# The SSD layer of a three-block fp32 kernel: ScalarE's slot re-ordered, the C B products and the causal product moved ahead, a GpSimd DMA moved to the head of its slot

## The reference, cut

```python
z, xbc, dt = jnp.split(h @ w_in, ...)
xbc = jax.nn.silu(causal_depthwise_conv(xbc, conv_w, conv_b))
xs, b_in, c_in = jnp.split(xbc, ...)
dt = softplus(dt + dt_bias); a = -jnp.exp(a_log)
a_cs = jnp.cumsum(dt * a)                       # per head, over tokens
decay = jnp.exp(where(causal, a_cs[l] - a_cs[s], -inf))
cb = einsum('bclgn,bcsgn->bcgls', c_c, b_c)     # C B, one per group
y = einsum(cb * decay, xs * dt) + ... + xs * d_skip
g = y * jax.nn.silu(z)
g = g * rsqrt(mean(g * g, over the group) + EPS) * norm_g
out = g @ w_out
```

## Time and profile before

| | |
|---|---|
| median of 3 runs | 1184.22 us (1183.47 to 1185.12) |
| the profiled execution, its own time | 1182.7 us |
| its span, first to last instruction | 1181.0 us |
| TensorE busy | 1124.5 us (95%) |
| VectorE, ScalarE, GpSimd busy | 761.9 (65%), 673.3 (57%), 164.9 us (14%) |
| TensorE's mean granted clock | 0.986 of full speed |
| first layer's slots 0 to 7 | from about 26 to 224 us |
| weight stream | 343 loads of 512 KB, 3.3 us to landing (median) |
| `acs_bc` loads by GpSimd | 8 of 544 KB, 4.8 us to landing (median) |

### The profile page before, as it was taken

How to read it: one execution, slowest core, us unless ns; L and a number is a source line. 1 busy time by engine, 2 the same in 40 slices (tenths; PEclk the granted TensorE clock), 3 DMA queues, 4 the chain that set the end, 5 groups by cost and what they waited for, 6 DMA issues and landing times.

```text
span 1181.0 us, 23759 instructions
## 1 busy us (share of the span) xinstructions
PE 1124.5 (95%) x8898; PEld 1078.7 (91%) x8898; DVE 761.9 (65%) x1119; ACT 673.3 (57%) x1071; POOL 164.9 (14%) x122
## 2 busy tenths in 40 slices
PE   6999999999999999789889999999999999999998
PEld 5888988889999999676579999999998999999998
DVE  4788777857665555458848665555688677666453
ACT  4788887755555443478736555444554656555332
POOL 0434354226100000300002000000001212000000
PEclk8999999999999999989989999999999999999999
DMA  5554434384555555322216555565543555655552
GB/s 194 178 176 152 144 132 155 140 231 166 179 176 178 170 170 176 125 72 92 88 37 195 183 190 183 176 195 176 170 157 127 176 184 173 196 180 192 183 189 93
DMA packets 53225, 190.32 MB, mean 161 GB/s; under 512 B 5920, under 2 KB 7072, under 8 KB 53168
## 3 DMA queue, kind: packets, MB, share of 16 engines
q1 hardware_dynamic: 51408, 182.95, 46.6%
q0 software_dynamic: 1760, 6.59, 1.8%
HBM read 188.44 MB, written 1.08 MB: 160 GB/s over the span
## 4 chain that ended last, share of the span: by engine, by line
PE 73%; issue 10%; DVE 8%; ACT 5%; POOL 3%; DMA 1%; POOLq 0%; ACTq 0%; DVEq 0%; SPq 0%
PE lin L412 23%; PE lin L414 23%; PE lin L413 22%; DVE w_lo L1221 2%; POOL w_lo L1753 2%; ACT w_hi L835 1%; POOL y L1771 1%; DVE cv L1300 1%; PE lin L643 1%; PE ps L445 1%; PE lin L645 1%; ACT pr L1109 0%; DMA acs_bc<-acs_dram 0%; ACT pr L1148 0%; DVE sg L1310 0%
## 5 line engine op out<-in xcount | busy, mean ns | idle before, releaser
L1221 DVE TENSOR_TENSOR w_lo<-w_raw,w_hi 128x1024 fp32r<-128x1024 f32 (+2 forms) x319 | 396.0, 1243 | 282.6 <-ACT w_hi L835 282.5
L835 ACT ACTIVATE w_hi<-w_raw 128x1024 fp32r<-128x1024 f32 (+1 forms) x343 | 354.4, 1040 | 248.6 <-PE lin L414 245.8
L412 PE MATMUL lin<-x_hi,w_hi 128*128 128x256 f32 (+1 forms) x1528 | 444.5, 291 | 11.0 <-DVE x_lo L1247 3.7
L414 PE MATMUL lin<-x_hi,w_lo 128*128 128x256 f32 (+1 forms) x1528 | 438.3, 287 | 0.0
L413 PE MATMUL lin<-x_lo,w_hi 128*128 128x256 f32 (+1 forms) x1528 | 437.6, 286 | 0.0
L412 PEld LDWEIGHTS lin<-x_hi,w_hi 128*128 128x128 f32 x1528 | 291.3, 191 | 15.1 <-DVE x_lo L1247 4.1
L413 PEld LDWEIGHTS lin<-x_lo,w_hi 128*128 128x128 f32 x1528 | 290.8, 190 | 1.4 <-issue 1.0
L414 PEld LDWEIGHTS lin<-x_hi,w_lo 128*128 128x128 f32 x1528 | 291.6, 191 | 0.0
L414 PE MATMUL lin<-hid_hi,w_lo 128*128 128x256 f32 (+1 forms) x768 | 218.2, 284 | 0.0
L413 PE MATMUL lin<-hid_lo,w_hi 128*128 128x256 f32 (+1 forms) x768 | 217.9, 284 | 0.0
L412 PE MATMUL lin<-hid_hi,w_hi 128*128 128x256 f32 (+1 forms) x768 | 217.4, 283 | 0.0
(11 more groups left out here) (251 smaller groups left out, 1481.1 us busy)
## 6 DMA issues: line engine op xcount, KB each, us to landing
w_raw<-w SPq DMA_DIRECT2D x343, 512.0 KB, 3.3
acs_bc<-acs_dram POOLq DMA_DIRECT2D x8, 544.0 KB, 4.8
bias_mask<-rpb POOLq DMA_DIRECT2D x4, 512.0 KB, 10.1
h<-h SPq DMA_DIRECT2D x4, 272.0 KB, 4.3
out<-h SPq DMA_DIRECT2D x8, 128.0 KB, 3.2
cst<-const SPq DMA_DIRECT2D x1, 784.0 KB, 8.8
vecs<-vec SPq DMA_DIRECT2D x1, 131.5 KB, 2.2
acs_dram<-y POOLq DMA_DIRECT2D x1, 34.0 KB, 2.2
```

The lines of the kernel that those rows point to most:

```text
L412: mm3(o, wh, xh, start=first and i == 0, stop=False)
L414: ins = mm3(o, wl, xh, start=False, stop=last and i == kts - 1)
L835: a(w_hi[pg.slot][:, 0:n], w_raw[pg.slot][:, 0:n], ACT.Copy).then_inc(w_hi_done, pages)
L1221: tt(w_lo[pg.slot][:, 0:n], w_raw[pg.slot][:, 0:n], w_hi[pg.slot][:, 0:n].bitcast(F32), ALU.subtract)\
```

## The change

On TensorE the C B products of a running slot are issued before the x transposes. On ScalarE the slot begins with the decay exponentials and the z sigmoid; `conv0` of xs stands between the two `w_hi` of chunk c+2; the square `h_sq` follows the second; the first half of `decay_logs` stands ahead of the xs sigmoid (in slots 1 to 7), the second half ahead of `w_hi` (c+4,0); `w_hi` (c+3,0) stands behind the xs sigmoid; the B C sigmoid stands ahead of `g_hi`. On VectorE the causal product stands ahead of the xs convolution, and the silu of xs ahead of `w_lo` (c+3,0). On GpSimd the DMA of the logarithms stands at the head of the slot. No instruction is added or removed.

```diff
@@ TensorE slot @@
                 if has_scan:
+                    cb_products(s + (-1))
                     x_transposes(s + (-1))
-                    cb_products(s + (-1))
@@ ScalarE slot @@
-                if has_lin:
-                    hi((c + 2).page(0))
-                    hi((c + 2).page(1))
                 if has_scan:
                     decay(g, 0)
                     decay(g, 1)
+                    kz = g.times(3, K_GRP + 2)
+                    act.wait_ge(drained[kz.parity], kz.half + 1)
+                    sigmoid(z_sg[:, :, :], zg_step, g.times(3), z_raw[:, :, :])
+                if has_lin:
+                    hi((c + 2).page(0))
+                    conv0(s, 0)
+                    hi((c + 2).page(1))
                 if has_stat:
                     act.wait_ge(y2_done, (gs + 1).value)
                     a(h_sq[:, 0:2, :], y2[:, :, :], ACT.Square).then_inc(ysq_done, 1)
                 if has_lin:
-                    conv0(s, 0)
-                    hi((c + 3).page(0))
+                    if s.base:
+                        decay_logs(s, 0)
                     act.wait_ge(clamped, s.times(2, 1).value)
                     sigmoid(sg[:, 0:2, :], sg_step, s.times(6))
-                if has_scan:
-                    kz = g.times(3, K_GRP + 2)
-                    act.wait_ge(drained[kz.parity], kz.half + 1)
-                    sigmoid(z_sg[:, :, :], zg_step, g.times(3), z_raw[:, :, :])
-                if has_lin:
+                    hi((c + 3).page(0))
                     conv0(s, 1)
                     hi((c + 3).page(1))
                 if not has_lin:
                     hi2(s + (C_SOUT - 6))
-                if has_lin and s.base:
-                    decay_logs(s, 0)
...
                 if has_lin:
+                    if s.base:
+                        decay_logs(s, 1)
                     hi((c + 4).page(0))
+                    act.wait_ge(clamped, s.times(2, 2).value)
+                    sigmoid(sg[:, 2:4, :], sg_step, s.times(6, 3))
...
                 if has_lin:
-                    act.wait_ge(clamped, s.times(2, 2).value)
-                    sigmoid(sg[:, 2:4, :], sg_step, s.times(6, 3))
                     if not s.base:
                         decay_logs(s, 0)
-                    decay_logs(s, 1)
+                        decay_logs(s, 1)
                     hi((c + 4).page(1))
@@ VectorE slot @@
                 if has_lin:
                     lo((c + 2).page(0))
+                    if has_scan:
+                        causal_cb(g)
                     conv(s, 0)
...
                 if has_scan:
                     scaled_tokens(g)
-                    causal_cb(g)
+                    if not has_lin:
+                        causal_cb(g)
...
                 if has_lin:
+                    silu(s, 0, xs_s[s.parity][:, :, :], cv[:, 0:2, :], sg[:, 0:2, :])
                     lo((c + 3).page(0))
-                    silu(s, 0, xs_s[s.parity][:, :, :], cv[:, 0:2, :], sg[:, 0:2, :])
@@ GpSimd slot @@
+                if has_lin and s.base:
+                    acs_rows(s)
                 if has_stat:
...
                     lo((c + 2).page(1))
-                    if s.base:
-                        acs_rows(s)
                     lo((c + 3).page(1))
```

## The result

The changed kernel takes **1169.65 us** (median of 4, 1166.48 to 1169.99) against 1183.85 of the kernel before on the same chip (median of 4): a ratio of 0.9877, 95% interval 0.9853 to 0.9901. That is 14.2 us faster. The profiled execution took 1169.99 us, with a span of 1168.3; the one of before took 1182.7.

A forecast was written before the change was run, and what follows sets the result against it. TensorE was taken as the busy engine, waiting for cbm. From 1182.7 us: 13.9 off in the slots, 3.2 added at the start, 0.7 for low clock, 0.7 off in the tail gives 1172.0; plus 1.5 to the median, 1173.5, range 1169.8 to 1179.0.

The forecast's parts named there:

- The slot with no wait: Running slots on TensorE: 22.9 us less 0.1 of draining and refilling round the wait, so 22.8 us.
- the step from the profiled execution to the median: Whole kernel: the median of the runs lies 1.5 us above the profiled execution, so 1172.0 becomes 1173.5.
- The bound, and why cbm was late: SSD slots: TensorE waits 10.1 us in six waits for cbm, which stands on VectorE behind a convolution waiting for ScalarE's cv.
- The gain in the slots: Six running slots fall from 150.7 us to 22.8 each: 13.9 us gained, both low-clock stretches included.
- ScalarE ties with TensorE: Running slots: ScalarE's round takes 22.8 to 22.9 us, level with TensorE's 22.8.
- The clamp held by GpSimd's w_lo: VectorE's clamp in running slots falls inside GpSimd's w_lo, so the xs sigmoid starts about 6.0 us behind cv.
- The load at the head: GpSimd's DMA of the logarithms lands 4.8 us from issue, about 3.9 after end 0, wanted at 3.7: even.
- rival B: ScalarE becomes the bound, its load landing 2.5 us later or more VectorE operations held behind GpSimd: 1177 us; chance 0.16.
- The start: Slots 0 and 1: ScalarE's new order delays the convolutions whose banks TensorE wants; 3.2 us lost, bounds 1.4 to 4.5.
- The half of a low-clock stretch: Start: a 1.5 us low-clock stretch may follow the second TensorE wait; half taken, 0.7 us lost, bounds 0 and 1.5.
- The tail: Slot 8: the z sigmoid goes ahead of the square and two waits of 0.35 us go; 0.7 us gained.
- rival C: The start costs nothing, as TensorE's lag gives ScalarE room, and no low clock comes: 1169.6 us; chance 0.05.

The follow-up runs named there:

- e1: Kernel before with only TensorE's and VectorE's part of the change, silu of xs in its old place: 1183.32 us against 1181.82.
- e2: Changed kernel with C B, transposes and causal product put back, silu of xs still ahead of w_lo (e2_scalar_only): 1174.31 us.
- e6: Changed kernel with one more ScalarE page instruction (0.95 us, result unused) in each of slots 2 to 7: 1172.96 us against 1168.99.
- after_again: The changed kernel run once more, unedited: 1168.99 us, beside 1181.28 of the kernel before on that chip.
- e8: Changed kernel with GpSimd's first w_lo, page (3,1), ahead of its DMAs of the logarithms at the start: 1169.04 us against 1168.99.

## Why the prediction missed its range, point by point

The two largest errors are of size. The slot with no wait was put at 22.8 us and measured 22.6, which is 1.15 us in six slots. And the step from the profiled execution to the median was put at 1.5 us up and measured 0.3 down, which is 1.8. By how little the range was missed, 0.15 us, is within the noise. The forecast of 1173.5 is a ratio of 0.9910 to 1184.2: the first measurement's interval ends at 0.9901, the repeat's reaches 0.9912. The firmer number is the gain between the marks, 12.8 us where the terms add up to 10.7.

- **The bound, and why cbm was late: right as far as it went, and not far enough.** I read the chain cbm, convolution, `cv`, `h_sq`, product. But I did not add up ScalarE's round of before, and did not ask what waits next when cbm alone is moved. e1 shows both: a ScalarE round of 24.9 us, and nearly the same 10 us under other names (8.2 us in six waits for `cv` inside the slots, 1.1 in four for y_sum). In the sum this did no harm, as the change also shortens that round; e2 shows that this part alone brings 9.7 of the 12.8 us.
- **The slot with no wait: 22.8 forecast, 22.6 measured.** This is the term of the mechanism that failed: I took 0.1 us for draining and refilling round a wait, and it is about 0.3. The rows give more. Before, the last matmul of the chunk starts at 106.07 and the statistic would start 0.13 later, at 106.20; it started at 108.29, 2.09 later for an idle time of 1.93. The next chunk then came 0.37 behind the statistic's start (108.66), where it is 0.26 after (83.30 and 83.56). Together 0.27 a wait. The earlier trace rows could have told the half of it: the pair of matmuls behind a wait took 0.73 us, the pair without one (L484) 0.62. Two other figures agree. The 15.05 us below, less 10.1 of idle time and 2.8 of low clock, leave 0.35 for each of six waits. And e2_scalar_only, whose statistic shows waits of only 0.17 us, has slots 0.44 longer.
- **The gain in the slots: 13.9 forecast, 15.05 measured** (first y products of slot 1 to those of slot 7, 150.73 us before and 135.68 after). The two low-clock stretches of the slots went with the waits, as assumed.
- **ScalarE ties with TensorE: right.** Round 22.72 against 22.60; e6 makes the tie visible. The clamp held by GpSimd's w_lo was forecast with its size (6.0 us from `cv` to the sigmoid, measured 6.08).
- **The load at the head: right.** It landed in 4.6 to 5.1 us. ScalarE waits 0.85 us for it, where I had it even; this lies inside the time that it would wait for the clamp, so it costs nothing. The rule in the Trainium skill ("SBUF — State Buffer", the box in "SBUF: two separate sides") on GpSimd's DMAs next to VectorE, beside which rival B's 1177 stood, does not show in these landings. But they do not test it either: in slots 1 to 7 of the changed kernel no clamp runs during the load's issue. The evidence is before's, as in the prediction: in slots 2 to 7 a clamp of 0.44 us ran beside the issue, and the loads landed in 4.8 to 4.9 us.
- **The start: 3.2 forecast, 3.4 measured** (61.06 - 28.00 against 58.73 - 29.07). The half of a low-clock stretch, 0.7, did not come in the profiled execution. In after_again a stretch came behind the first of the two waits and cost nothing, hidden in the second wait as forecast; in e8 one came behind the second wait and cost 1.5.
- **The tail: 0.7 forecast, 1.2 measured**, the two short waits of 0.35 with, it seems, again more than their idle time; no run isolates this.
- **From one execution to the median.** Forecast for the profiled execution: 1172.0; measured 1170.0. The terms above give 1.15 + 0.5 + 0.7 - 0.2 = 2.1 of this; the head was 1.1 us shorter, and what follows the tail 1.2 us longer. The other 1.8 us of the miss is the conversion: before, the profiled execution was 1.5 us under the median, and I added that; after, it was 0.3 above. Which execution of three or four the profile fell on is luck. The untouched rest of the span varies by 5.5 us. A range built from the terms of the change alone, ending 3.7 us under the forecast, was too short on that side, and rival C (1169.6), which came nearest, was so for the wrong reason: the start was not free.

What stays open: when a wait of about 2 us is followed by a low-clock stretch. After waits of 2.13 us at the same place (the first mark) it came in some executions and not in others. In e1 it came after waits of 1.53 and 1.65 us and not after 1.56 and 1.64.

## What to carry to other kernels

When a wait is removed, list every other condition that the waiting engine meets in the same microseconds: here moving cbm alone gave nothing, since the same late ScalarE instruction held the next bank. Adding up each engine's round with its waits shows this beforehand. Once the busiest engine has no wait left, look at whose round ties with it, and at the warm-up of the pipeline, where the steady order can be the wrong one. And price a wait by the starts of the instructions on both sides, not by its idle time, and a forecast's range by how much the untouched part varies.

## What the runs showed of the hardware that I had not expected

- A VectorE clamp (`tensor_scalar`, fp32, both sides in SBUF) can be held by a GpSimd operation that by the profile starts after it: it began at 35.67 us, GpSimd's w_lo at 36.12, and the clamp ended at 38.83, behind the w_lo. GpSimd's DMA issue (35.43 to 36.02) ran when the clamp began. The issue alone does not hold it: in e8 a clamp beginning at 34.52, during the issue of the store of the logarithms, took its 0.45, and before, one beginning at 106.23, during the issue of a load (106.20), took 0.44. In both of these no w_lo followed the issue at once. The Trainium skill ("SBUF — State Buffer", "Who interferes with whom") gives the shared ports to the one that issues first; by the starts of clamp and w_lo it was the other, and no run here tells why.
- Two `g_lo`, both of whose inputs are in SBUF, take 0.91 us together before; in the changed kernel, beside GpSimd's w_lo (163.19 to 165.72), they take three times that, and 4.58 us in e2_scalar_only. VectorE waits for ScalarE afterwards anyway (1.64 us), so the changed kernel loses nothing by it:

```profile
162.95 3.07 DVE L1344 SCALAR_TENSOR_TENSOR g_lo<-z_s,vecs,g_hi 128x272 f32 x2
...
167.66 1.23 DVE L1221 TENSOR_TENSOR w_lo<-w_raw,w_hi 128x1024 fp32r<-128x1024 f32 x1 [1.64 <-ACT w_hi L835]
```

- A wait of TensorE for the statistic costs about 0.3 us more than its idle time (0.27 from the rows of one, 0.35 over the six), and a wait shown as 0.17 us cost 0.44.
